# The opening of a two-block kernel: unit 0 and half of X in quarters, squares from a second copy of X, the first group summed ahead of its root, constants asked for later

## What is computed

```python
# first block
h = rmsnorm(x, norm_mix);  p = h @ w_in                      # 2048 -> 4352
y_a = pool_mixer(p[:, :512]);  y_b = hyena(p[:, 512:2816]);  y_c = spatial_gating(p[:, 2816:])
x = x + concat(y_a, y_b, y_c) @ w_out
h = rmsnorm(x, norm_ffn);  gate, val = split(dwconv3(h @ ffn_w_up))
x = rmsnorm(x + (silu(gate) * val) @ ffn_w_down, norm_final)
# second block
h = fox_attention(rmsnorm(x, g0));  x = x + rmsnorm(h, g1)
h = square(relu(rmsnorm(x, g2) @ w1)) @ w2;  x = x + rmsnorm(h, g3)
```

## Time and profile before

| | us |
|---|---|
| median of 3 runs | 2201.43 |
| lowest and highest | 2201.28, 2202.84 |
| the profiled execution | 2201.5 |
| its span (first to last instruction) | 2199.7 |
| PE busy in the span | 2166.7 |
| VectorE, ScalarE, GpSimd busy | 1312.5, 1009.4, 51.2 |
| HBM read | 406.38 MB |

### The profile page before, as it was taken

How to read it: one execution, slowest core, us unless ns; L and a number is a source line. 1 busy time by engine, 2 the same in 40 slices (tenths; PEclk the granted TensorE clock), 3 DMA queues, 4 the chain that set the end, 5 groups by cost and what they waited for, 6 DMA issues and landing times.

```text
span 2199.7 us, 27911 instructions
## 1 busy us (share of the span) xinstructions
PE 2166.7 (99%) x11682; PEld 1860.2 (85%) x11682; DVE 1312.5 (60%) x1612; ACT 1009.4 (46%) x1181; POOL 51.2 (2%) x76
## 2 busy tenths in 40 slices
PE   7999999999999999999999999999999999999998
PEld 6788888888888888888898889878888888888886
DVE  7967547777676775444655565456555555444444
ACT  5444436555555544333554444445333334433333
POOL 1030000000000000000001010000000000000000
PEclk9999999999999999999999999999999999999999
DMA  9554655655555555555566555546666665555552
GB/s 311 161 177 156 210 186 178 201 182 192 192 191 192 191 188 185 187 189 189 156 217 195 170 173 186 188 129 215 187 189 189 192 191 191 188 186 187 189 190 95
DMA packets 267949, 410.30 MB, mean 187 GB/s; under 512 B 6645, under 2 KB 246325, under 8 KB 249392
## 3 DMA queue, kind: packets, MB, share of 16 engines
q1 hardware_dynamic: 264672, 395.47, 54.9%
q0 software_dynamic: 2432, 11.74, 1.5%
q10 hardware_dynamic: 720, 1.31, 0.2%
HBM read 406.38 MB, written 2.11 MB: 186 GB/s over the span
## 4 chain that ended last, share of the span: by engine, by line
PE 93%; DVE 3%; ACT 1%; issue 1%; DMA 1%; DVEq 0%; SPq 0%; ACTq 0%
PE bank L1382 33%; PE bank L1395 17%; PE bank L1419 11%; PE bank L1424 11%; PE bank L1420 11%; PE bank L1385 2%; PE bank L1386 2%; PE bank L1397 2%; DMA raw<-in_w_in 1%; ACT whi L405 1%; DVE wlo L692 1%; PE bank L1276 1%; PE bank L1230 0%; DVE M L1166 0%; PE bank L1363 0%
## 5 line engine op out<-in xcount | busy, mean ns | idle before, releaser
L692 DVE TENSOR_TENSOR wlo<-raw,whi 128x2048 fp32r<-128x2048 f32 (+1 forms) x374 | 857.2, 2293 | 790.7 <-ACT whi L405 790.7
L405 ACT ACTIVATE whi<-raw 128x2048 fp32r<-128x2048 f32 (+1 forms) x374 | 716.5, 1918 | 800.2 <-PE bank L1424 438.6
L1382 PE MATMUL bank<-hh,whi 128*128 128x512 f32 x3392 | 826.1, 396 | 16.6 <-ACT whi L405 10.9
L1382 PEld LDWEIGHTS bank<-hh,whi 128*128 128x128 f32 x3392 | 626.9, 189 | 148.5 <-ACT whi L405 10.9
L1395 PEld LDWEIGHTS bank<-hh,wlo 128*128 128x128 f32 x3392 | 429.7, 188 | 17.6 <-DVE wlo L692 0.4
L1395 PE MATMUL bank<-hh,wlo 128*128 128x256 f32 x3392 | 434.9, 281 | 0.0
L1419 PE MATMUL bank<-whi,hh 128*128 128x512 f32 x1088 | 428.8, 394 | 2.2 <-DVE M L855 2.2
L1420 PE MATMUL bank<-whi,hh 128*128 128x512 f32 x1088 | 427.5, 393 | 0.0
L1424 PE MATMUL bank<-wlo,hh 128*128 128x512 f32 x1088 | 274.3, 394 | 0.0
L1419 PEld LDWEIGHTS bank<-whi,hh 128*128 128x128 f32 x1088 | 204.5, 188 | 50.8 <-issue 2.4
L1424 PEld LDWEIGHTS bank<-wlo,hh 128*128 128x128 f32 x1088 | 204.3, 188 | 47.4
(11 more groups left out here) (225 smaller groups left out, 864.3 us busy)
## 6 DMA issues: line engine op xcount, KB each, us to landing
raw<-in_mlp_w SPq DMA_DIRECT2D x128, 1024.0 KB, 5.5
raw<-in_ffn_w_up SPq DMA_DIRECT2D x88, 1024.0 KB, 5.1
raw<-in_ffn_w_down SPq DMA_DIRECT2D x44, 1024.0 KB, 4.8
raw<-in_w_in SPq DMA_DIRECT2D x34, 1024.0 KB, 5.5
raw<-in_fox_w_in SPq DMA_DIRECT2D x32, 1024.0 KB, 5.3
raw<-in_fox_w_in SPq DMA_DIRECT2D x16, 1032.0 KB, 5.4
raw<-in_w_out SPq DMA_DIRECT2D x16, 1024.0 KB, 4.9
raw<-in_fox_w_out SPq DMA_DIRECT2D x16, 1024.0 KB, 4.7
```

What stands on the lines that cost most here:

```text
L405: e.activation(whi[i % RING][:, 0:n], raw[i % RAW][:, 0:n], ACT.Copy).then_inc(s_hi, 1)
L692: e.tensor_tensor(wlo[i % RING][:, 0:n], raw[i % RAW][:, 0:n], whi[i % RING][:, 0:n].bitcast(F), ALU.subtract).then_inc(s_lo, 1)
L1382: e.matmul(bank[b][:, :], wh[:, k, s], hh[:, kk, :], start=kk == 0, stop=False)
```

## The change

- **Unit 0 and half of X in quarters.** SyncE's queue loads unit 0 in four parts of 256 KB, ScalarE's queue the gains' first 16 columns (8 KB), X chunks 0 to 7 in four parts of 256 KB, and the rest of cols. ScalarE and VectorE take a quarter at a time: hi and lo of two chunks of X, then hi and lo of 512 columns of the unit. PE waits for each quarter (`s_hi0`, `s_lo0`). Unit 1 is split ahead of X chunks 8 to 15.
- **PE's first instructions** are 32 matmuls of 128 columns on the matrix of ones, into bank 7, which nothing reads.
- **Squares from a second copy of X.** `gx`, with tokens on partitions, is loaded in two transfers of 1 MB behind units 2 and 3 and ahead of unit 4. ScalarE squares each half in one instruction of 2048 columns with a running sum. The root is taken of two columns, and `diagonal` and `spread` make `rb`, as in the later norms. The additions of squares, `total` and the transposes are gone.
- **First group.** In `middle_tap` and `conv` of group 0, unit 4 is split behind the bank's sum and ahead of the product with `rb`; VectorE makes the sum of group 0 ahead of its wait for `rb`.
- **Filter work moved.** The two sines are cut in two entries (`angles` on VectorE, `sin` on ScalarE), the first filter matmul stands behind unit 1 instead of 3, the second behind unit 4 instead of 5. The second half of `filter3` and `filter4`, the turns and transforms stand one unit later.
- **Constants later.** w3, cs and the first half of decay are asked for when PE is through with three units, the layer norm's tables after seven, pool_w and edge after the transforms' products.

The diff, cut to its core:

```diff
 SIDE = {
-    1: [("split", 4), ("spread", 0)], 2: [("total", 0)], 3: [("filter1", 0)], 4: [("first_r", 0)], 5: [("filter2", 0)], 7: [("filter3", 0)],
-    9: [("filter4", 0)], 10: [("filter3", 1)], 12: [("filter4", 1)], 13: [("z_turn", 0)], 14: [("z_turn", 1)],
-    15: [("dft", 0)], 16: [("dft", 1)], 17: [("dft", 2)], 18: [("dft", 3)], 19: [("late", 0)],
+    0: [("angles", 0)], 1: [("filter1", 0), ("first_root", 0), ("sin", 0)], 3: [("spread", 0)], 4: [("filter2", 0), ("angles", 1)], 5: [("sin", 1)],
+    7: [("filter3", 0)],
+    9: [("filter4", 0)], 11: [("filter3", 1)], 13: [("filter4", 1)], 14: [("z_turn", 0)], 15: [("z_turn", 1)],
+    16: [("dft", 0)], 17: [("dft", 1)], 18: [("dft", 2)], 19: [("dft", 3)],
...
 def sync(e):
-            e.dma_start(X[:, 0:4, :], A["x"][:, 0:4, :]).then_inc(s_x[0], 16)
-            load(0)
-            e.dma_start(X[:, 4:8, :], A["x"][:, 4:8, :]).then_inc(s_x[1], 16)
+            src = units[0][0]
+            for m in range(4):
+                e.dma_start(raw[0][:, 512 * m:512 * m + 512].rearrange("p (k c) -> p k c", k=2), src[:, 2 * m:2 * m + 2, :]).then_inc(
+                    s_w0[m] if m < 3 else s_raw[0], 16)
             load(1)
-            e.dma_start(X[:, 8:12, :], A["x"][:, 8:12, :]).then_inc(s_x[2], 16)
-            e.dma_start(X[:, 12:16, :], A["x"][:, 12:16, :]).then_inc(s_x[3], 16)
-            for i in range(2, NU):
+            e.dma_start(X[:, 8:12, :], A["x"][:, 8:12, :]).then_inc(s_x[4], 16)
+            e.dma_start(X[:, 12:16, :], A["x"][:, 12:16, :]).then_inc(s_x[5], 16)
+            load(2)
+            load(3)
+            for h in range(2):
+                e.dma_start(gx[:, h, :], A["xt"][:, h, :]).then_inc(s_xh[h], 16)
+            for i in range(4, NU):
                 load(i)
...
 def gpsimd(e):
-            for dst, src in ((fe[0:33, :], A["feat"]), (f1, A["filt"]), (w3, A["w3"]), (CS, A["cs"]), (wpool, A["pool_w"])):
+            for dst, src in ((fe[0:33, :], A["feat"]), (f1, A["filt"])):
+                e.dma_start(dst, src).then_inc(s_feat, 16)
+            e.wait_ge(s_unit, 3)
+            for dst, src in ((w3, A["w3"]), (CS, A["cs"])):
                 e.dma_start(dst, src).then_inc(s_const, 16)
...
 def scalar(e):    # middle_tap; conv on VectorE has split(4) and spread_out(1) in the same place
                 for n in range(2):
                     small_terms(pair + n, conv_tiles(kind, j, n)[3]).then_inc(s_cvs, 1)
+                if cg == 0:
+                    split(4)
...
-                    if what == "spread":
-                        root(1, rb[:, :])
+                    if what == "first_root":
+                        for h in range(2):
+                            e.wait_ge(s_xh[h], 16)
+                            e.activation(gx[:, h, :], gx[:, h, :], ACT.Square, accum_out=ss_x[:, h:h + 1]).then_inc(s_sqx, 1)
+                        root(1, rstd)
...
-            e.dma_start(cols[:, :], A["cols"]).then_inc(s_col, 16)
+            e.dma_start(cols[:, 0:KD], A["cols"][:, 0:KD]).then_inc(s_gmix, 16)
+            for q in range(4):
+                e.dma_start(X[:, 2 * q:2 * q + 2, :], A["x"][:, 2 * q:2 * q + 2, :]).then_inc(s_x[q], 16)
+            e.dma_start(cols[:, KD:NCOL], A["cols"][:, KD:NCOL]).then_inc(s_col, 16)
             e.wait_ge(s_ones, 1)
             sqrt_table()
+            e.wait_ge(s_gmix, 16)
+            for q in range(4):
+                s = slice(512 * q, 512 * q + 512)
+                e.wait_ge(s_x[q], 16)
+                high(q, "mix")
+                e.wait_ge(s_w0[q] if q < 3 else s_raw[0], 16)
+                e.activation(whi[0][:, s], raw[0][:, s], ACT.Copy).then_inc(s_hi0 if q < 3 else s_hi, 1)
+            done[0] = 1
+            split(1)
+            for q in range(4, 8):
+                e.wait_ge(s_x[2 + q // 2], 16)
+                high(q, "mix")
             e.wait_ge(s_col, 16)
...
 def tensor(e):
+            e.wait_ge(s_ones, 1)
+            for _ in range(32):
+                e.matmul(bank[7][:, 0:P], onesr[:, :], onesr[:, :], start=True, stop=True)
```

More of the change, by code:

```diff
@@ L230, in two_block_program @@
         s_hi, s_lo, s_unit = sem("s_hi"), sem("s_lo"), sem("s_unit")
-        s_x = [sem(f"s_x{q}") for q in range(4)]
+        s_x = [sem(f"s_x{q}") for q in range(6)]
+        s_xh = [sem(f"s_xh{h}") for h in range(2)]
+        s_w0 = [sem(f"s_w0{m}") for m in range(3)]
+        s_hi0, s_lo0, s_gmix, s_feat, s_pw = (sem(n) for n in ("s_hi0", "s_lo0", "s_gmix", "s_feat", "s_pw"))
         s_col, s_id, s_const, s_decay, s_ft, s_edge, s_ln, s_bs, s_again, s_fox = (
@@ L359, in gpsimd @@
             e.wait_ge(s_pq, 8)
+            e.dma_start(wpool, A["pool_w"]).then_inc(s_pw, 16)
+            e.dma_start(edge[:, :], A["edge"]).then_inc(s_edge, 16)
             for i in range(4):
@@ L572, in joined @@
                     square_sum(stage, h, Xt[:, h, :], h)
-            e.dma_start(cols[:, :], A["cols"]).then_inc(s_col, 16)
+            e.dma_start(cols[:, 0:KD], A["cols"][:, 0:KD]).then_inc(s_gmix, 16)
+            for q in range(4):
+                e.dma_start(X[:, 2 * q:2 * q + 2, :], A["x"][:, 2 * q:2 * q + 2, :]).then_inc(s_x[q], 16)
+            e.dma_start(cols[:, KD:NCOL], A["cols"][:, KD:NCOL]).then_inc(s_col, 16)
             e.wait_ge(s_ones, 1)
             sqrt_table()
-            e.wait_ge(s_col, 16)
[L578 to L589, removed]
+            e.wait_ge(s_gmix, 16)
[10 more added lines that the diff above has]
+                high(q, "mix")
+            e.wait_ge(s_col, 16)
             for g, (kind, j, _) in enumerate(IN_GROUPS):
                 i, b = U_IN + 2 * g, 2 * (g % 2)
-                group(i, ahead=(kind, j) != ("gu", 2))
+                group(i, ahead=g and (kind, j) != ("gu", 2))
                 if kind in ("x1", "v", "x0"):
@@ L967, in side @@
                 for what, n in SIDE.get(i, ()):
-                    if what == "spread":
-                        e.wait_ge(s_tot, 1)
-                        root(1, bank[7][:, 0:T], 1.0 / D, RMS_EPS, rb[:, :])
+                    if what == "first_root":
+                        e.wait_ge(s_sqx, 2)
+                        root(1, ss_x, 1.0 / D, RMS_EPS, rstd)
+                        e.wait_ge(s_rcp, 1)
+                        e.wait_ge(s_id, 16)
+                        diagonal(rstd)
                     elif what == "up_r":
@@ L1075, in joined @@
                 turned(3, gname)
-            e.wait_ge(s_col, 16)
[L1078 to L1083, removed]
-                if q == 5:
-                    split(1)
-            split(2)
-            for q in range(2, 8):
-                add_square(q)
+            e.wait_ge(s_gmix, 16)
+            for q in range(4):
+                s = slice(512 * q, 512 * q + 512)
+                e.wait_ge(s_x[q], 16)
+                low(q, "mix")
+                e.wait_ge(*((s_hi0, q + 1) if q < 3 else (s_hi, 1)))
+                e.tensor_tensor(wlo[0][:, s], raw[0][:, s], whi[0][:, s].bitcast(F), ALU.subtract).then_inc(s_lo0 if q < 3 else s_lo, 1)
+            done[0] = 1
+            split(1)
+            for q in range(4, 8):
+                e.wait_ge(s_x[2 + q // 2], 16)
+                low(q, "mix")
+            e.wait_ge(s_col, 16)
             for g, (kind, j, _) in enumerate(IN_GROUPS):
                 i, b = U_IN + 2 * g, 2 * (g % 2)
-                group(i, ahead=(kind, j) != ("gu", 2))
+                group(i, ahead=g and (kind, j) != ("gu", 2))
                 if kind in ("x1", "v", "x0"):
-                    if g == 0:
-                        e.wait_ge(s_rcp, 1)
                     conv(kind, j, b, group_done(U_IN, g))
@@ L1280, in side @@
                 for what, n in SIDE.get(i, ()):
-                    if what == "total":
-                        e.wait_ge(s_ones, 1)
-                        e.wait_ge(s_sumd, 7)
-                        e.matmul(bank[7][:, 0:T], ones, acc[:, 0:T], start=True, stop=False)
-                        e.matmul(bank[7][:, 0:T], ones, acc[:, T:2 * T], start=False, stop=True).then_inc(s_tot, 1)
+                    if what == "spread":
+                        spread(1)
                     elif what == "up_r_out":
                         e.wait_ge(s_lx, 32)
-                        spread(1)
+                        spread(2)
                     elif what == "both_r_out":
                         e.wait_ge(s_lx, 48)
-                        spread(2)
+                        spread(3)
                     elif what == "filter1":
-                        e.wait_ge(s_const, 80)
+                        e.wait_ge(s_feat, 32)
                         e.matmul(bank[4][0:64, 0:T], f1[0:33, 0:64], fe[0:33, :], start=True, stop=True).then_inc(s_fmm, 1)
-                    elif what == "first_r":
-                        e.wait_ge(s_id, 16)
-                        e.wait_ge(s_rcp, 1)
-                        by_token()
                     elif what == "filter2":
```

66 lines of the change are left out of this document (28 added, 38 removed).

## The result

| | before | after |
|---|---|---|
| median, us | 2201.43 | 2193.23 |
| lowest and highest of 5 | 2201.22, 2204.55 | 2192.52, 2194.14 |
| profiled execution, its span | 2201.5, 2199.7 | 2194.14, 2192.3 |

The ratio is 0.9958 [0.9944, 0.9971]: the change makes the kernel faster by 8.2 us between the medians, 6 to 12 us by the interval. The forecast was 2195.6, a gain of 5.8 on that median. The sign was right, the gain too small. Before's five executions here were also short ones: its 43 later executions, on three chips, have a median of 2203.07.

A forecast was written before the change was run, and what follows sets the result against it. PE, busy 99% of the span, bounds the kernel, its opening a race of byte stream and engines. Unit 4 at 34.6 and 3.94 us of waits gone give 5.9 us: 2201.5 - 5.9 = 2195.6, range 2192.7 to 2199.9.

The forecast's parts named there:

- The opening: Start to unit 4: unit 0 from 6.4 to 13.5, unit 1 at 15.0, unit 4 at 34.6 against 36.57 before.
- Its chain from landing to PE: Ahead of unit 4: copy of X lands at 27.8, then square, root, sine, small terms, unit 4's copy, to 34.5.
- unit 4 earlier: End of the opening: PE starts unit 4 at 34.6 instead of 36.57, 1.97 us.
- waits of PE for VectorE gone: Unit 4 to unit 16: PE's waits for banks or filter results from VectorE vanish, 3.94 us.
- transposes and rest up to the inverse transform: Behind unit 4: the removed transposes of 128 columns on PE, taken at nothing.
- case 2: Unit 4: the copy of X comes early and PE binds at 32.9, 1.7 us more gain, 2193.9; chance 0.17.
- case 1: The forecast: unit 4 waits for the copy's chain, starting between 34 and 35.5; 2195.0 to 2196.5, center 2195.6; chance 0.48.
- All behind is PE at 99% with the same work, so the 5.9 us last to the end: Behind unit 16: PE's work is unchanged, so the 5.9 us gained by there stay to the end.
- shows no fall later: PE's clock: the trace agrees with a slow start at 1.2 GHz, with no later fall.
- Theory A: Formed after the result: unit 4 earlier and VectorE's waits gone as predicted; the excess is clock stretches behind PE's waits.
- Rival B: Against Theory A: the excess comes from a part priced at nothing (ones matmuls, quarters, filter order); no chance given.
- Case 3: Opening: quarters slow the stream, 2.1 MB at 266 instead of 371 cost 2.2 us, unit 4 at 36.8, 2197.8; chance 0.15.

## Why the prediction came out as it did

The opening held, step by step. Unit 1 began at 14.90 (15.0), unit 3 at 26.91 (27.0), the second wide square at 27.50 (27.8), unit 4 at 34.07 (34.6). Its chain from landing to PE took 6.57 us (6.8). PE waited 1.0 us there (1.7): the spread ended at 33.1, as walked (32.9). VectorE's waits are gone to the last tenth. Only unit 0 missed. Its first matmul came at 7.88 against 6.4: the 32 ones took 7.09 us, 0.22 each, and the queue was held by them; even without them unit 0 began at 7.07. It ended at 14.8 against 13.5, its hi pass taking 5.10 us where unit 1's took 3.96. As predicted, neither cost anything, for unit 1 was waiting for its own load.

The terms of the gain, between the profiled executions and then to the medians:

| | predicted | measured |
|---|---|---|
| unit 4 earlier | 1.97 | 2.50 |
| waits of PE for VectorE gone | 3.94 | 3.94 |
| transposes and rest up to the inverse transform | 0 | 0.2 |
| before's clock at half behind its 1.8 us wait | 0 | 1.6 |
| after's clock at half behind its 2.2 us wait (1.3), less 0.4 regained to the end | 0 | -0.9 |
| from the profiled executions to the medians | -0.1 | 0.8 |
| sum | 5.8 | 8.2 |

The gain is 2.4 us over the sum, by about 0.5 in unit 4's start (the copy of X came 0.3 earlier and the chain behind it was 0.2 shorter), 0.2 in the transposes, 0.7 net in the clock, and 0.9 between the profiled executions and the medians. The time comes out nearest to case 2's 2193.9, but by case 1's mechanism: unit 4 waited for the copy of X and began at 34.07, so case 2 was not what happened.

The step that failed is "All behind is PE at 99% with the same work, so the 5.9 us last to the end". It is true of the work and not of its speed: two stretches at half clock, 1.6 us in before and 0.9 net in after, were put at nothing. The prediction asked of the clock whether the opening was slow, and read "shows no fall later" off the stages in front of 122 us alone. That reading was wrong: two slices of the same trace from 202 to 206 us show 0.55 and 0.59. Behind each wait of about 2 us that PE has in this kernel, the clock may or may not fall, and it costs 1.1 to 1.6 us when it falls for 3.4 us, and 4.8 when it falls for 10.2. In the fourteen profiles the 1.8 us wait has a fall behind it in four, the 2.2 us wait near 240 in seven, never both in one profile, and three have neither. The wait at the filter was therefore worth its 2.2 us and a chance of 4.8 more, and the change took away both. That chance is no part of the 8.2: the profile that the table uses has no fall there, and only four of 43 executions are long enough to have had the long one. That no clock falls there after is seen in all eleven profiles of kernels that have no such wait; of three profiles of before, two show the fall.

Theory A holds for the pair of profiles, where the clock is half of the 1.4 us of excess; for the medians it is not shown. Rival B fell: neither part priced at nothing (ones matmuls, filter order) holds the excess, and the quarters' 1.9 us are in the opening as predicted. Case 3, a stream made slower by quarters, fell on the earlier trace rows against 264 and 374 GB/s. The Trainium skill (DMA: Bandwidth & Descriptors, "Bandwidth") gives a 64 KB transfer less than half the rate of one of 1 MiB; this trace shows that eight of 256 KB in flight on two queues move as much as the larger ones did.

What stays open: whether the last 0.8 us of the table is the fall at 235.7 missing from after's other four executions (2192.52 to 2193.51, where the profiled one took 2194.14). Its price of 1.1 us fits, but those executions have no trace. Larger, and as open, is what lies in before's usual execution: against its later median of 2203.07 the gain is near 9.8 us, and after without the ones was 9.2 under before on one chip. So some 2 us beyond the 7.4 between the profiles are in no trace, and that the forecast lay 2.4 off and not 4 owes something to before's short five. Nor do these runs show what decides whether the clock falls behind one and the same wait, or between 3.4 us and 10.2 us.

## What to carry to other kernels

Where TensorE is busy nearly all the time, price a wait that goes or comes at its length and at the clock stretch that may follow it, and look for such stretches over the whole span, not only where the change is. Before shortening a chain, name the next load behind it: here 1.0 of the 1.4 us by which unit 4 came earlier ran into unit 5's load. A wait with two cures is not worth two gains.

## What was not expected of the hardware

- The 32 matmuls of 128 columns at the start took 0.22 us each (7.09 in all), where one with four times the columns took 0.43 us at the slow start. The Trainium skill (TensorE: Matmul & The Clock Gate, "Wait — 56ns, not 53.3ns?") gives 107 ns from start to start for 128 columns on the cold array; the trace has twice that, for matmuls that each load their weights. They brought unit 0's hi pass from 6.11 to 5.10 us and held its start back by 0.8; of the 0.2 left nothing reaches unit 1, which waits for its load.
- The granted clock falls to half behind waits of 1.8 to 3.5 us, for 3.4 us or (before, twice) for 10.2, with PE busy all along; each fall begins within 1.6 us of the wait's end. The same wait has it in one execution and not in the next.
